# Borders between layers in column chunks, and part of w_ada summed on TensorE in strips

## What is computed

```python
c_act = jax.nn.silu(c)
for l in range(2):
    mod = c_act @ w_ada[l] + b_ada[l]                 # 2048 x 6144, one row
    shift, scale, gate = jnp.split(mod, 3, axis=-1)
    h = _layernorm(x) * (1.0 + scale[:, None, :]) + shift[:, None, :]
    p = h @ w_in[l]                                   # 2048 x 3904
    ...                                               # Fourier mixing and attention
    y = jnp.concatenate([y_f, y_a], axis=-1) @ w_out[l]
    x = _layernorm(DEEPNORM_ALPHA * x + gate[:, None, :] * y, ln_g[l], ln_b[l])
# layers 2 (even) and 3 (odd)
h = rms_norm(x, norm_g) @ w_in
...
x = x + y @ w_out
```

## Time and profile before

| | |
|---|---|
| median of three runs | 1708.89 us (1707.84 to 1715.83) |
| profiled execution | 1710.67 us, of which span 1708.9 us |
| mean granted TensorE clock | 0.957 of full speed |
| PE busy | 1535.3 us, 90% of the span |
| DVE busy | 1081.6 us, 63% |
| ACT busy | 688.9 us, 40% |
| moved by DMA | 342.94 MB, mean 201 GB/s |

### The profile page before, as it was taken

How to read it: one execution, slowest core, us unless ns; L and a number is a source line. 1 busy time by engine, 2 the same in 40 slices (tenths; PEclk the granted TensorE clock), 3 DMA queues, 4 the chain that set the end, 5 groups by cost and what they waited for, 6 DMA issues and landing times.

```text
span 1708.9 us, 25051 instructions
## 1 busy us (share of the span) xinstructions
PE 1535.3 (90%) x9839; PEld 1340.9 (78%) x9839; DVE 1081.6 (63%) x1835; ACT 688.9 (40%) x1173; POOL 58.2 (3%) x86
## 2 busy tenths in 40 slices
PE   4899899888966999999986999989998899999998
PEld 0667678887746878998865998879886798888986
DVE  3435677888786734666766457794655747877553
ACT  1333224324223432534434444454544445655442
POOL 3000000000000000000000000000002500000000
PEclk8899999999987999999997999999998899999999
DMA  9995778997863755776564545325564463334563
GB/s 352 380 379 175 248 253 287 320 328 268 280 225 100 247 147 168 245 244 210 186 191 150 167 137 167 117 87 173 162 207 146 133 182 111 110 101 140 176 218 108
DMA packets 184070, 342.94 MB, mean 201 GB/s; under 512 B 28972, under 2 KB 47632, under 8 KB 183184
## 3 DMA queue, kind: packets, MB, share of 16 engines
q1 hardware_dynamic: 179920, 326.88, 59.3%
q0 software_dynamic: 4032, 14.46, 2.5%
HBM read 339.14 MB, written 2.15 MB: 200 GB/s over the span
## 4 chain that ended last, share of the span: by engine, by line
PE 70%; DVE 11%; DMA 9%; ACT 6%; issue 3%; SPq 1%; DVEq 0%; POOLq 0%; POOL 0%; ACTq 0%
PE PM L1315 58%; PE PB L1315 8%; DMA stg<-in_w_in 4%; DVE wlo L1887 2%; DMA stg<-in_w_out 2%; ACT whi L1609 2%; ACT AR L1609 2%; DVE X L1811 1%; SPq L1237 1%; DMA AR<-in_w_in 1%; DVE AC L1811 1%; DMA stg<-in_w_ada 1%; PE PB L1461 1%; PE PB L1536 1%; ACT TMP L1609 1%
## 5 line engine op out<-in xcount | busy, mean ns | idle before, releaser
L1887 DVE TENSOR_TENSOR wlo<-stg,whi 128x1024 fp32r<-128x1024 f32 (+3 forms) x412 | 486.0, 1190 | 365.7 <-ACT whi L1609 362.4
L1609 ACT ACTIVATE whi<-stg 128x1024 fp32r<-128x1024 f32 (+3 forms) x412 | 419.7, 1025 | 503.7 <-PE PM L1315 321.8
L1315 PE MATMUL PM<-Hh,whi 128*128 128x256 f32 x1824 | 533.7, 293 | 21.7 <-DVE wlo L1887 21.3
L1315 PE MATMUL PM<-Hl,whi 128*128 128x256 f32 x1824 | 521.8, 286 | 0.0
L1315 PE MATMUL PM<-Hh,wlo 128*128 128x256 f32 x1824 | 521.4, 286 | 0.0
L1315 PEld LDWEIGHTS PM<-Hh,whi 128*128 128x128 f32 x1824 | 354.4, 194 | 45.8 <-DVE wlo L1887 30.6
L1315 PEld LDWEIGHTS PM<-Hl,whi 128*128 128x128 f32 x1824 | 354.5, 194 | 0.4
L1315 PEld LDWEIGHTS PM<-Hh,wlo 128*128 128x128 f32 x1824 | 354.4, 194 | 0.0
L1315 PE MATMUL PM<-whi,Hh 128*128 128x512 f32 (+1 forms) x704 | 278.9, 396 | 17.9 <-DVE wlo L1887 11.8
L1315 PE MATMUL PM<-whi,Hl 128*128 128x512 f32 (+1 forms) x704 | 273.1, 388 | 0.0
L1315 PE MATMUL PM<-wlo,Hh 128*128 128x512 f32 (+1 forms) x704 | 273.0, 388 | 0.0
(11 more groups left out here) (240 smaller groups left out, 1276.2 us busy)
## 6 DMA issues: line engine op xcount, KB each, us to landing
stg<-in_w_ada SPq DMA_DIRECT2D x153, 512.0 KB, 5.3
stg<-in_w_in SPq DMA_DIRECT2D x104, 512.0 KB, 5.2
stg<-in_even_w_in SPq DMA_DIRECT2D x80, 512.0 KB, 3.6
stg<-in_w_out SPq DMA_DIRECT2D x64, 512.0 KB, 5.2
stg<-in_odd_w_in SPq DMA_DIRECT2D x64, 512.0 KB, 3.7
AR<-in_w_ada SPq DMA_DIRECT2D x39, 512.0 KB, 11.5
stg<-in_even_w_out SPq DMA_DIRECT2D x32, 512.0 KB, 4.1
stg<-in_odd_w_out SPq DMA_DIRECT2D x32, 512.0 KB, 4.7
```

Of the source, the lines that this page charges most:

```text
L1315: return e.matmul(out, l, r, start=start, stop=stop, skip_group_check=True)
L1609: return e.activation(out, x, f, **k)
L1887: e.tensor_tensor(wlo[s["lo"]][:, :, 0:n], stg[s["slot"]][:, :, 0:n], whi[s["hi"]][:, :, 0:n].bitcast(F32), ALU.subtract).then_inc(SEM["lo ...
```

## The change

- `gate_pe` sums layer 0's gate on PE: two groups of 16 tiles of 128 rows by 1024 columns, whose two halves go to strips of one bank (`strips`, views "both"). ACT copies the bank to AC, and `adap_row` spreads it over the partitions, with `SEL` as selector.
- `ada_pe(1, 3)` sums columns 1536 to 2047 of layer 1's shift and scale on PE, 16 tiles. They lie in the job list around w0 to w4 of layer 1: ten before w0, two after each of w1, w2 and w3. Their columns are made (`columns`) ahead of w4's matmuls.
- The other 80 tiles (32 of the gate, 48 of layer 1's shift and scale) lie evenly over the rest of layer 0, from five jobs earlier on, and none among the last six jobs.
- `lead` has a `first`, which runs before the preparation of the current job, and a `more`, one per job. The normed Z is written in four chunks of 512 columns (`xn`); before the first job stand two of them and three chunks of transposes, and each of the next five jobs brings one chunk of transposes.
- In these first eight jobs PE takes Hh by whi and wlo for both blocks first, then Hl by whi. Chunk 0 goes from PSUM to Hh on ACT at once; its TMP and Hl follow on DVE.
- After layer 0 ACT takes the first half's sum and sum of squares while DVE works on the second half; the second X pass is cut in two halves of 1024 columns. After layer 1 ACT takes four squares of 1024 columns instead of eight of 512.
- The stationary columns of a strip are columns k to k+31 of `CAX`, of which the first is used and the rest is ignored, in place of a zero-filled `CZ`.

```diff
+            j = self.jobs[i - AHEAD] if i >= AHEAD else {}
+            if j.get("first"):
+                j["first"]()
...
+    def strips(self, srcs, views, done):
         st, out = {}, []
...
+        for n, (src, (a, b)) in enumerate(zip(srcs, views)):
+            def body(job, n=n, a=a, b=b):
+                if n % 2 == 0:
+                    st["other"] = job
+                    if n == 0:
+                        st["bank"], st["free"] = self.now(self.banks)
+                    return
+                other = st["other"]
+                mm = self.tick("adap_mm")
+                self.step("adap", first=n == 1, last=n == len(srcs) - 1, k=n // 2 * 2, bank=st["bank"],
+                          free=st["free"] if n == 1 else (), slots=[other["slot"], job["slot"]], ld=[other["ld"], job["ld"]],
+                          views=[views[n - 1], (a, b)])
+                self.stgs.put(other["slot"], mm)
+                self.stgs.put(job["slot"], mm)
+                if n == len(srcs) - 1:
+                    st["a"], afree = self.now(self.accs)
+                    st["ev"] = self.tick("adap_out")
+                    self.step("adap_out", bank=st["bank"], mm=mm, a=st["a"], free=afree)
+                    self.banks.put(st["bank"], st["ev"])
+                    if done:
+                        done(st)
+            out.append(dict(mode="pe", src=[src], n=src[1], mm=body))
+        return out, st
...
+        srcs = [(0, 512, f"w_ada{l}", n // 2 * 2, n % 2 * D + g * 512) for n in range(KT)]
+        out, st = self.strips(srcs, [("rows", n % 2) for n in range(KT)], None)
...
+    def gate_pe(self, l, n0):
+
+        c0 = 2 * D + n0
+
+        def rows(st):
+            mm = None
+            for g in range(2):
+                b, fr = self.now(self.banks)
+                mm, u = self.tick("ada_mm"), self.tick("gate_row")
+                gg = n0 // 512 + g
+                self.step("adap_row", bank=b, free=fr, a=st["a"], ev=st["ev"], mm=mm, half=g, gg=gg,
+                          r=48 * l + 32 + 4 * gg, gate_free=self.gate_free[gg])
+                self.gate[gg] = u
+                self.banks.put(b, u)
+            self.accs.put(st["a"], mm)
+        return self.strips([(0, 1024, f"w_ada{l}", k, c0) for k in range(KT)], [("both", k % 2) for k in range(KT)], rows)[0]
...
+    def normed(self, cs):
+        for c in cs:
+            self.step("xn", c=c, z_free=self.z_free, **self.norm)
+            self.xn[c] = [self.tick("xn0"), self.tick("xn1")]
...
+    def lead(self, first, trans, layer):
+
         n = len(self.jobs)
         begin = layer()
 
...
+        def lead():
+            first()
+            self.normed((0, 1))
+            trans((0, 1, 2))
             begin()
-        self.jobs[n]["pre"] = both
+
+        def more(q):
+            if q < 3:
+                self.normed((q + 1,))
+            trans((q + 2,))
+            if q == 5:
+                self.zw = self.h[KT - 1]
+        self.jobs[n]["first"] = lead
+        for q in range(8):
+            self.jobs[n + q]["fresh"] = True
+        for q in range(1, 6):
+            self.jobs[n + q]["pre"] = lambda q=q: more(q)
...
+        gate = []
+        for n in (0, 1024):
+            gate += self.gate_pe(0, n)
+        rest = []
+        for c0, n in ((0, 1024), (D, 1024), (1024, 512), (D + 1024, 512)):
+            rest += self.ada(1, c0, n)
+        ex = [j for n in range(16) for j in (rest[3 * n], gate[2 * n], rest[3 * n + 1], gate[2 * n + 1], rest[3 * n + 2])]
+        self.interleave(n0 - 5, ex, len(ex), len(self.jobs) - n0 - 1)
+
+        def norm1():
+            p = self.post_norm(0)
+            self.ln(p["out"][3], p)
+
+        n1 = self.lead(norm1, lambda qs: self.mod_h(1, qs), lambda: self.mla(1))
+        late, columns = self.ada_pe(1, 3)
+        w = self.jobs[n1:]
+        more = w[4]["pre"]
+
+        def last_chunk():
+            columns()
+            more()
+        w[4]["pre"] = last_chunk
+        self.jobs[n1:n1 + 5] = late[:10] + w[0:2] + late[10:12] + w[2:3] + late[12:14] + w[3:4] + late[14:16] + w[4:5]
+        n1 += 16
...
-        self.interleave(n1 + 4, ex, 72, 32)
...
+        self.interleave(n1 + 6, ex, 70, 32)
+
+        def norm2():
+            p = self.post_norm(1)
+            self.rms(p["squared"], p["ss"], 4)
+
+        self.lead(norm2, lambda qs: self.transposed("en", None, qs), self.even)
...
+                    for kk in range(2) if s["h_hi"] else ():
+                        k = 2 * s["q"] + kk
+                        q.wait_ge(s["h_hi"][kk])
+                        opened = set()
+                        for u in s["units"]:
+                            b = PM[2 * s["pair"] + u["bk"]]
+                            first = k == 0 and u["bk"] not in opened
+                            opened.add(u["bk"])
+                            for W in (H, L):
+                                w = W[:, kk, u["c0"]:u["c0"] + u["n"]]
+                                if u["kind"] == "A":
+                                    mm(b[0:u["n"], u["off"]:u["off"] + S], w, Hh[:, k, :], first and W is H, False)
...
+                    for kk in range(2) if s["h_hi"] else ():
+                        k = 2 * s["q"] + kk
+                        q.wait_ge(s["h"][kk])
+                        for u in s["units"]:
+                            b = PM[2 * s["pair"] + u["bk"]]
+                            w = H[:, kk, u["c0"]:u["c0"] + u["n"]]
+                            if u["kind"] == "A":
+                                ins = mm(b[0:u["n"], u["off"]:u["off"] + S], w, Hl[:, k, :], False, k == KT - 1)
...
+                        k = s["k"] + i
                         for half in range(2):
+                            if s["views"][0][0] == "rows":
+                                x = stg[s["slots"][half]][:, i, :]
+                            else:
+                                x = stg[s["slots"][i]][:, half, :]
                             o = 64 * half + 32 * i
-                            ins = mm(B[o:o + 32, :], CZ[:, k, :], stg[s["slots"][half]][:, i, :], s["q"] == 0, s["q"] == KT // 2 - 1)
+                            ins = mm(B[o:o + 32, :], CAX[:, k:k + 32], x, s["first"], s["last"])
...
+                elif kind == "adap_row":
+                    q.wait_all(s["free"])
+                    q.wait_ge(s["ev"])
+                    q.wait_ge(const)
+                    mm(B[:, :], bcast(SEL[:, s["half"]:s["half"] + 1], 128), acc_of(dict(a=s["a"], n=512), 0), True, False)
...
+                    if s["q"] == 0:
+                        q.wait_ge(s["mm"])
+                        q.wait_all(s["need"])
+                        q.wait_ge(s["h_free"])
+                        for k in range(2):
+                            pin = B[:, k * S:(k + 1) * S]
...
+                elif kind == "xn":
+                    cols = slice(512 * s["c"], 512 * s["c"] + 512)
+                    q.wait_ge(s["ready"])
                     q.wait_ge(s["z_free"])
...
+                    if s["how"] == "ln":
+                        ins = act(XN[:, 1, cols], X[:, 1, cols], ACT.Identity, bias=sm(s["nb"], 1), scale=sm(s["y"] + 1, 1))
+                    else:
+                        ins = act(XN[:, 1, cols], X[:, 1, cols], scale=sm(s["y"] + 1, 1))
+                    ins.then_inc(SEM["xn1"], 1)
+                elif kind == "post_norm" and s["l"] == 0:
                     q.wait_ge(s["z_free"])
...
+                    q.wait_ge(s["out"][1])
+                    act(XN[:, 0, :], X[:, 0, :], accum_out=sm(s["sum"], 1)).then_inc(SEM["pn_sum"], 1)
+                    q.wait_ge(s["summed"])
+                    act(sm(s["nm"], 1), sm(s["sum"], 1), scale=-1.0 / D).then_inc(SEM["pn_mean"], 1)
+                    q.wait_ge(s["mean"])
+                    act(XN[:, 0, :], X[:, 0, :], ACT.Square, bias=sm(s["nm"], 1), accum_out=sm(s["sq"], 1)).then_inc(SEM["pn_sq"], 1)
...
+                        if s["q"] == 0:
+                            q.wait_ge(s["hh"])
...
-                        stt(X[:, t, :], X[:, t, :], y[:, t:t + 1], ar(D, D), ALU.mult, ALU.add).then_inc(SEM["post_norm"], 1)
+                        for o in (0, 1024):
+                            x = X[:, t, o:o + 1024]
+                            stt(x, x, y[:, t:t + 1], ar(D + o, 1024), ALU.mult, ALU.add).then_inc(SEM["post_norm"], 1)
```

249 lines of the change are left out of this document (119 added, 130 removed).

## The result

The changed kernel takes 1746.14 us, median of four runs (1741.82 to 1748.69), and the kernel before beside it 1708.37; the ratio is 1.0211, 95% interval 1.019 to 1.0232. The forecast was 1712, range 1699 to 1726: **wrong, 34 us too low and outside its range.** The profiled execution has a span of 1745.7.

What follows compares the result with a forecast made beforehand. The prediction took PE, busy 90% of the span, as the bound, with time to gain only where it stands or runs at half clock. +2, +11, -4.5 and -5 sum to +3.5 on the 1708.89 median: 1712 us, range 1699 to 1726.

Steps and rivals of the forecast that it cites:

- A: Spread w_ada work, second layer-0 projection to end of w_out: PE visits and waits against removed stalls, +2 us.
- On the path since PE is the bound: Layer 0's w_ada stretch: 16 gate strip visits at 0.65 us add their full 10.4 us.
- rival (2): Layer 0 stretch: tiles held for PE starve the slot ring, stalls stay and w_out waits grow; 1728 us, chance 0.20.
- B: Border between layers 0 and 1: later norm start, shorter way to first matmul, work behind it, column wait; +11 us.
- the w_out waits of 9.3 rise by half: Layer 0's w_out jobs, part of rival (2): PE's 9.3 us of waits grow, adding 5 us.
- Strips at 0.45 us a visit: PE's strip visits: four matmuls of 512 columns take 0.45 us, with entering and leaving 0.65 us.
- rival (4): Strip visits cost double, 0.9 us at four passes; 19 visits add 8.6 us, 1721 us, chance 0.02.
- rival (1): Between 270 and 497 all 26 us of stalls and lost clock go; 1698 us, chance 0.17.
- the wait for the columns: Border 0 to 1: PE waits 4.6 us for ACT's copy of the strips' sum before columns 12 to 15.
- C: Border between layers 1 and 2: split off the path, fewer squares, earlier first matmul; -4.5 us.
- D: Border between layers 2 and 3: alternating splits and chunks, first group ends 21.5 us after the norm; -5 us.
- the two signs that I named for being wrong: w1's tile landed by 8 us at border 0 to 1, or new SyncE waits for strip sums in w_out jobs.

Runs made afterwards that it cites:

- number 2: Changed kernel with layer 0's gate summed on VectorE instead of PE, even placing and late tiles kept; 1709.41 us, ratio 0.9999.
- number 9: number 2 with the slots of 32 w_ada tiles put back into the rotation only where PE's visit would stand, no visit made; 1735.59 us, ratio 1.0157.
- number 5: number 2 with 16 extra PE visits of four matmuls on a constant, holding no tile and no bank; 1712.09 us, ratio 1.0018.
- number 7: number 2 with four slots for weight tiles instead of five in the whole kernel; 1746.63 us, ratio 1.023.
- numbers 3: Changed kernel with seven of each eight gate strip visits cut to 32 of 512 columns, tiles held as long; 1739.44 us, ratio 1.0173.
- number 1: Changed kernel with only the new borders: w_ada work summed on VectorE, placed as before the change, no late tiles; 1697.99 us, ratio 0.9932.
- number 14: Changed kernel with GpSimd's 32 mask additions of the odd layer cut from 256 columns to 16; 1731.27 us, ratio 1.012.
- number 6: number 2 with one shared PSUM bank out of use from the 4th to 40th and 44th to 80th w_ada tile; 1712.33 us, ratio 1.0022.
- number 13: Changed kernel with seven slots, three split buffers of each kind and work prepared two jobs ahead; 1732.88 us, ratio 1.0131.
- number 12: number 11 with seven slots, three split buffers of each kind and work prepared two jobs ahead, not three; 1720.31 us, ratio 1.0055.
- number 15: number 11 with GpSimd's 32 odd-layer mask additions held back until layer 3's second group of matmuls is done; 1686.12 us, ratio 0.9868.
- number 11: number 1 with all 96 w_ada tiles, summed on VectorE, spread evenly over the jobs; 1695.43 us, ratio 0.9927.

## Why the prediction was wrong

**A, the step that failed:** PE was taken for the bound of the stretch ahead of border 0 to 1, and what the held tiles do to the ring of slots was put at nothing in the sum. A was forecast at +2 and was +29.1. By the kernels above, each by its A, this is -4.6 (placing and fewer tiles, number 2), +26.2 (rotation, number 9 less number 2), +7.5 (what PE's visits add to that, the changed kernel less number 9).
- *"On the path since PE is the bound"* was the wrong sentence. The page's 90% and a stretch like the earlier trace rows made me take PE for the bound with stalls on it. There the ring of slots sets the pace: 16 us of PE work cost at most some 3 us of the kernel (number 5), a slot less 37 (number 7).
- *The ring.* I named the mechanism as rival (2), with the right place, and in B I even followed stg3 through w1, w2, w3 and w4. In A I priced it by the stalls that I knew, +16, and gave it 0.20; it was +33.7 between number 2 and the changed kernel. The rule I made there (it decides when a pair is held longer than a turn of the slots) was wrong too: nothing has to be late. A slot that is dealt out later makes the others come round after three or four loads from the first pair on, whatever the clock says. This stood in the order of the loads, where I looked only at the border. The sentence "the w_out waits of 9.3 rise by half" had no ground: 13.1 of the 29.1 us are lost before layer 0's long run of w_in, where my sum has only the visits' own time.
- *The number of tiles.* I wrote 0.9 w_ada tiles a job until six jobs before the end of w_out, and none among the last six. In SyncE's order it is nearly one to one, and the last thirteen w_out tiles have none beside them: `interleave` is called with 80 as its number of jobs and 83 as its number of tiles.
- *Strips at 0.45 us a visit.* A visit is 1.06:

```profile
143.69 0.28 PE L1372 MATMUL PM<-Hh,wlo 128*128 128x256 f32 x1
143.90 1.06 PE L1372 MATMUL PB<-stg,CAX 128*32 128x512 f32 x8
144.90 0.38 PE L1372 MATMUL PM<-Hh,whi 128*128 128x256 f32 x1
```

  Eight records, four calls. A call on plain fp32 (the strips) leaves two records in the trace, one on fp32r (the split tiles) leaves one: the 2560 calls of whi with Hh have 2560. So the 24 records of the earlier trace rows were three visits of 0.9, not six. The trace of before had the means to see it: its strip groups count 156 and 100 records, and 32 visits of four calls are 128 calls.

```profile
L1315 PE MATMUL PB<-AR,RX 128*32 128x512 f32 x156 | 27.5, 689 | 3.8 <-DMA AR<-in_w_ada 3.8
L1315 PE MATMUL PB<-stg,RX 128*32 128x512 f32 x100 | 21.5, 786 | 14.7 <-DMA stg<-in_w_ada 13.5 <-DMA AR<-in_w_ada 1.1
```

  Four strips side by side in 0.9 us are four times the 0.227 of one pass of 512 columns. The Trainium skill, FP8 and Floating Point Precision, TensorE Precision Notes, says that true FP32 takes four passes through the array: the trace agrees with it, and rival (4), to which I gave 0.02, was right on the size. The prediction's "here the trace disagrees with it" came from my misreading of the row. On the time of the kernel it decided little (numbers 3 and 5), since the ring set the pace. A slip besides: the sum of rival (1) is 1697, not 1698.

**B was right** in its sum (+11; +12.2) and in the steps that rows show: the late aggregate (15; 16.4), the first matmul (36; 37.0), the wait for the columns (4.6; 3.5). The late tiles are dear all the same: without them the border gains where it now costs (number 1).

**C was right** (-4.5; -4.6).

**D: the step was right, a term mis-sized.** -5 was forecast, -1.2 came. The count of 21.5 us, where 26.8 came, went by DVE's times while GpSimd is idle (0.69 for 512 columns); beside its additions they are 1.22, and with the additions cut the group took 21.0 (number 14). The additions stand in the trace of before too, which I had not asked for GpSimd there:

```profile
1319.34 15.18 POOL L1301 TENSOR_TENSOR AR<-AR 128x256 f32<-128x256 f32 x16 [6.55 <-DMA AR<-in_consts]
```

My 1.7 us for handovers was a guess in the right direction for the wrong reason.

**The signs.** PE's waits for wlo should have fallen to 3; from 280 to 407 they are

```profile
PE PM L1372 <- DVE wlo L2002: 10.0, 7, 2.9
```

against the 13.2 of the earlier trace rows. Of the two signs that I named for being wrong, neither came: w1 landed late as forecast, and SyncE hardly waited for PE. In the w_out jobs (407 to 526) it waited for none of PE's work. It waited for DVE's splits, 221.1 us from 147 to 520. I had looked for the ring to fail at the tile held, and it fails at the others.

**Left open:** why PE's visits cost 7.5 us on top of the rotation (the changed kernel less number 9) and nothing in number 5 (less number 2). PE's own account from 147 us to A says where the two differ. In both the visits add 16 to 17 us of work and PE's idle time falls by 9.9; but what is lost at 1.2 GHz (half of each such stretch) falls by 8.5 in number 5 and rises by 1.7 in the changed kernel. That is an account and not yet a cause. All of the difference is there when the long run of w_in begins: at 268.3 in the changed kernel, 259.0 in number 9, 256.1 in number 2, 259.9 with the bank held (number 6) and 254.1 with seven slots (number 13). Open is also the last +1.2 us in layer 3, and what of number 12's loss comes from the split buffers and what from the job ahead.

## What to carry to other kernels

Before a step is moved to another engine, ask how long it will keep its buffers *in the order in which the program deals them out*: count for each load how many loads ago its buffer was last used, before and after. Here about half of the loads came round after three or four in place of five, and that cost 26 us, where 16 us of work added on PE cost about 3. The count warns; it doesn't give the price (number 9). And an engine that is busy nine tenths of a stretch isn't the bound of that stretch for being so: a dummy operation of known length, added in one kernel, tells.

## What the runs showed of the hardware

- **DVE beside GpSimd.** Operations with two SBUF inputs (Hl from TMP and Hh, wlo from stg and whi, 512 columns) take 1.22 us while GpSimd runs its additions, 0.69 without; Z of 512 columns from X, one input, takes 0.48 without (1305.72 in number 15) and 0.95 beside it (1363.08 in the changed kernel). Operations that read PSUM (TMP from PB) stayed at 0.43 each. The Trainium skill, GPSIMD Engine Reference, Specifications, says that the SBUF interfaces are shared with VectorE, with contention for DVE instructions in a 2-port mode or with two SBUF inputs. The trace agrees on the two inputs, at a factor of 1.8; whether Z with its one input runs in such a mode, no run here shows. Moving the additions out of layer 3's first two groups gave 9 us (number 15 against number 11).
- **Plain fp32 matmuls** appear as two records a call, and four in strips of 32 columns take the time of four passes, 0.9 us for 512 columns.
- **The clock.** From 147 to 490 the granted clock has a mean of 0.97 in number 2 and of 0.99 with 16 us of added matmuls in it (number 5). In number 2 it is at 1.2 GHz in place of 2.4 six times there, 23.8 us in all, each time beginning within 1.5 us of the end of a wait of PE of 2.3 to 3.5 us. In number 5 it is so once, for 6.8 us, at a wait of 3.5. PE was busy only 10 us more for 16 us of added work, so filling its waits gave back part of the price.
